# A two-block transformer kernel in split fp32: the feed-forward norm's factor applied after the products instead of before

## What is computed

```python
def rmsnorm(x, g):
    xf = x.astype(jnp.float32)
    y = xf * lax.rsqrt(jnp.mean(xf * xf, axis=-1, keepdims=True) + EPS)
    return (y * g.astype(jnp.float32)).astype(x.dtype)
...
        x = x + merged @ w_o[l]

        h = rmsnorm(x, norm_ffn_g[l])
        gt, up = jnp.split(h @ w_ffn_in[l], 2, axis=-1)
        x = x + (jax.nn.silu(gt) * up) @ w_ffn_out[l]
```

## Time and profile before

| | us |
|---|---|
| median of 3 runs | 1573.46 |
| lowest, highest | 1570.94, 1575.38 |
| the profiled execution, its time | 1571.23 |
| the profiled execution, its span | 1569.4 |

### The profile page before, as it was taken

How to read it: one execution, slowest core, us unless ns; L and a number is a source line. 1 busy time by engine, 2 the same in 40 slices (tenths; PEclk the granted TensorE clock), 3 DMA queues, 4 the chain that set the end, 5 groups by cost and what they waited for, 6 DMA issues and landing times. The chain is left out here.

```text
span 1569.4 us, 25089 instructions
## 1 busy us (share of the span) xinstructions
PE 1524.5 (97%) x10118; PEld 1342.1 (86%) x10118; DVE 1149.5 (73%) x1497; ACT 819.5 (52%) x1113; POOL 131.5 (8%) x119
## 2 busy tenths in 40 slices
PE   7999999999999999999998989999999999999998
PEld 6999889999799988999987678887888888878887
DVE  6798678786678867878569777777878766766665
ACT  6464454444646445444468755445656565655442
POOL 2060000000113000000004000000111102000000
PEclk9999999999999999999999999999999999999999
DMA  9765366666775646667632247766887765346652
GB/s 327 263 222 202 134 232 229 205 239 240 249 269 202 203 134 232 201 218 274 236 128 96 93 171 269 259 223 193 288 289 251 267 168 187 108 150 211 211 171 102
DMA packets 223762, 327.42 MB, mean 209 GB/s; under 512 B 12216, under 2 KB 175520, under 8 KB 223648
## 3 DMA queue, kind: packets, MB, share of 16 engines
q1 hardware_dynamic: 216584, 315.11, 59.6%
q10 hardware_dynamic: 7064, 10.71, 1.9%
HBM read 316.32 MB, written 9.47 MB: 208 GB/s over the span
## 5 line engine op out<-in xcount | busy, mean ns | idle before, releaser
L1768 DVE TENSOR_TENSOR wparts<-raw,wparts 128x2048 fp32r<-128x2048 f32 (+1 forms) x240 | 545.7, 2279 | 209.7 <-ACT wparts L1285 209.5
L1285 ACT ACTIVATE wparts<-raw 128x2048 fp32r<-128x2048 f32 (+1 forms) x240 | 454.5, 1897 | 118.9 <-PE bank L566 86.3
L564 PE MATMUL bank<-hT,wparts 128*128 128x256 f32 x1216 | 349.1, 287 | 1.7 <-DVE hT L1869 1.5
L565 PE MATMUL bank<-hT,wparts 128*128 128x256 f32 x1216 | 344.3, 283 | 0.0
L566 PE MATMUL bank<-hT,wparts 128*128 128x256 f32 x1216 | 344.3, 283 | 0.0
L564 PEld LDWEIGHTS bank<-hT,wparts 128*128 128x128 f32 x1216 | 233.1, 192 | 6.3 <-issue 6.0
L565 PEld LDWEIGHTS bank<-hT,wparts 128*128 128x128 f32 x1216 | 233.4, 192 | 0.2
L566 PEld LDWEIGHTS bank<-hT,wparts 128*128 128x128 f32 x1216 | 233.3, 192 | 0.0
L564 PE MATMUL bank<-wparts,aT 128*128 128x512 f32 (+1 forms) x536 | 212.8, 397 | 0.7 <-DVE aT L1849 0.5
L565 PE MATMUL bank<-wparts,aT 128*128 128x512 f32 (+1 forms) x536 | 208.0, 388 | 0.0
L566 PE MATMUL bank<-wparts,aT 128*128 128x512 f32 (+1 forms) x536 | 207.7, 388 | 0.0
(11 more groups left out here) (284 smaller groups left out, 1882.3 us busy)
## 6 DMA issues: line engine op xcount, KB each, us to landing
raw<-in_mlp_w SPq DMA_DIRECT2D x64, 1024.0 KB, 5.5
ada_raw<-in_ada_w SPq DMA_DIRECT2D x96, 512.0 KB, 6.4
raw<-in_w_ffn_in SPq DMA_DIRECT2D x44, 1024.0 KB, 5.3
raw<-in_w_in SPq DMA_DIRECT2D x43, 1024.0 KB, 5.7
raw<-in_dil_w_in SPq DMA_DIRECT2D x64, 512.0 KB, 4.9
raw<-in_w_ffn_out SPq DMA_DIRECT2D x22, 1024.0 KB, 5.3
raw<-in_w_o SPq DMA_DIRECT2D x8, 1024.0 KB, 5.0
biasb<-head_bias ACTq DMA_DIRECT2D x16, 512.0 KB, 6.6
```

The costliest lines, as they stand in the source:

```text
L564: pe.matmul(dst, held[:, 0, :], streamed[:, 0, :], start=start, stop=False)
L565: pe.matmul(dst, held[:, 0, :], streamed[:, 1, :], start=False, stop=False)
L1285: act.activation(view(whi[c % SPL], c), view(raw[c % RAW], c), ACT.Copy).then_inc(s_hi, 1)
L1768: dve.tensor_tensor(view(wlo[c % SPL], c), view(raw[c % RAW], c), view(whi[c % SPL], c).bitcast(F32), ALU.subtract).then_inc(s_lo, 1)
```

## The change

Per feed-forward layer of the first block:

- The norm's factor is no longer applied to x. TensorE transposes plain `x` (`raw_block`): columns 0 to 511 before output chunk 3, columns 512 to 1023 of token half 0 behind it, of token half 1 inside the first gate chunk (`first_gate`, `upper_blocks`). `hT` holds x times the gain.
- The factor is still formed from the same squares, but later in each engine's program. TensorE spreads it over all partitions with two small matmuls between the halves of the first up chunk (`spread_rstd`), and VectorE copies it into `rstd_rows`.
- Gate: ScalarE copies the sum out of PSUM (Copy in place of Silu), VectorE multiplies it by `rstd_rows` in SBUF, ScalarE takes Silu in place. The up sum is not scaled; the missing factor enters at the final addition, a `scalar_tensor_tensor` in place of a `tensor_tensor`.
- The transposes and sums use other PSUM banks, so that none is written before it is free.
- SyncE's wait ahead of the seven small loads is on the factor (`s_rstd`) in place of normed x.

```diff
@@ -803,13 +805,57 @@
                 four_for_weights()
+
+                def raw_block(k, t, b=None):
+                    nm = ("nrm", 2 * l + 1, k)
+                    if b is not None:
+                        begin("a", nm, freed_by=(s_hlo, low_done(2 * l + 1, k // 2)), b=b)
+                    return pe.transpose(bank[jobs[nm][2]][:, P * t:P * t + P], x[:, t, P * k:P * k + P], ident[:, :])
+
                 for c in range(4):
                     out_half, half = divmod(c, 2)
+                    if c == 0:
+                        sums, turned = list(rings["w"]), list(rings["a"])
+                    if c == 3:
+                        for t in range(TT):
+                            emptied(pe, ("WO", l, 0, t))
+                        for k in range(DK // 2):
+                            raw_block(k, 0, turned[k])
+                            end(raw_block(k, 1), ("nrm", 2 * l + 1, k))
                     w = weights(("WO", l, c))
                     wide_half(("WO", l, out_half), ("WO", l, c), w, half, None if out_half else ("mg", l))
-                three_for_weights()
-                norm(2 * l + 1, xnf)
+                emptied(pe, ("WO", l, 1, 0))
+                for k in range(DK // 2, DK):
+                    raw_block(k, 0, (sums[0], sums[1], turned[0], turned[1])[k - DK // 2])
+                rings.update(w=[sums[2], sums[0], sums[1]], a=[turned[2], turned[3], sums[3], turned[0], turned[1]])
+                n.update(w=0, a=0)
                 accs = None
+
+                def upper_blocks():
+                    emptied(pe, ("WO", l, 1, 1))
+                    for k in range(DK // 2, DK):
+                        end(raw_block(k, 1), ("nrm", 2 * l + 1, k))
+
+                def first_gate(name, w):
+                    bk = begin("w", name)
+                    for ks in (range(DK // 2), range(DK // 2, DK)):
+                        for i in range(2):
+                            for k in ks:
+                                await_pair(("nrm", 2 * l + 1), i, k)
+                                m = mm3(bk[:, S * i:S * i + S], w[:, :, k, P * i:P * i + P], hT[:, :, k, :],
+                                        (i, k) == (0, 0), (i, k) == (1, DK - 1))
+                            if (i, k) == (0, DK // 2 - 1):
+                                upper_blocks()
+                    end(m, name)
+
+                def spread_rstd():
+                    at = RSTD_OF[2 * l + 1]
+                    pe.wait_ge(s_rstd, at + 2)
+                    bk = begin("a", ("rstd", l))
+                    for t in range(TT):
+                        m = pe.matmul(bk[:, P * t:P * t + P], rstd[:, (at + t) % 2, 0:1].broadcast_to([P, P]), ident[:, :],
+                                      start=True, stop=True)
+                    end(m, ("rstd", l))
 
...
@@ -828,8 +874,10 @@
                             w = weights((nm, l, c))
-                            feature_major((nm, l, c), w, (0, P), hT, 0, DK,
-                                          first_of=None if c or i else ("nrm", 2 * l + 1))
+                            if c or i:
+                                feature_major((nm, l, c), w, (0, P), hT, 0, DK, between=idle if c else spread_rstd)
+                            else:
+                                first_gate((nm, l, c), w)
                             used((nm, l, c))
...
@@ -1137,7 +1185,7 @@
                     l = name[1]
-                    sp.wait_ge(s_xn, 2 * (2 * l + 1) + 2)
+                    sp.wait_ge(s_rstd, RSTD_OF[2 * l + 1] + 2)
                     for dst, a in ((posb[:, :], A["positions_2"][0:1, :].broadcast_to([96, S])), (thr[:, :], A["thr"]),
...
@@ -1494,11 +1538,22 @@
                         h_high(mg[:, 2 * kp:2 * kp + 2, :], hT_hi[:, 2 * kp:2 * kp + 2, :], 0.5)
-                for c in range(4):
+                def ffn_gain(k):
+                    return colA[:, c_ffn(l) + k:c_ffn(l) + k + 1]
+
+                def out_square(half, t):
+                    emptied(act, ("WO", l, half, t))
+                    square(2 * l + 1, 2 * half + t, sqf, t, half, 512 * half, 512 * half + 512)
+
+                for c in range(3):
                     split_ahead(("WO", l, c))
-                norm_sums(2 * l + 1, sqf)
-                norm_upper(2 * l + 1, xnf)
-                norm_high(2 * l + 1, lambda k: colA[:, c_ffn(l) + k:c_ffn(l) + k + 1])
+                out_square(0, 0)
+                out_square(0, 1)
+                norm_high(2 * l + 1, ffn_gain, range(DK // 2))
+                split_ahead(("WO", l, 3))
+                out_square(1, 0)
+                norm_high(2 * l + 1, ffn_gain, range(DK // 2, DK))
+                out_square(1, 1)
 
...
@@ -1524,10 +1579,12 @@
                             emptied(act, ("UP", l, c - 2))
-                        act.activation(sg[c % 2][:, :, :], bk[:, :].rearrange("p (a s) -> p a s", a=2), ACT.Silu)\
+                        act.activation(sg[c % 2][:, :, :], bk[:, :].rearrange("p (a s) -> p a s", a=2), ACT.Copy)\
                            .then_inc(drain_sem(("GT", l, c)), 1)
                         split_ahead(("UP", l, c))
                         stage_biases(u0)
+                        act.wait_ge(s_scaledgate, NF1 * l + c + 1)
+                        act.activation(sg[c % 2][:, :, :], sg[c % 2][:, :, :], ACT.Silu).then_inc(s_silu, 1)
                         emptied(act, ("UP", l, c))
...
@@ -2094,20 +2151,25 @@
                 split_ahead(("AO", l, 1))
+                def ffn_gain(k):
+                    return colA[:, c_ffn(l) + k:c_ffn(l) + k + 1]
+
                 for c in range(3):
                     split_ahead(("WO", l, c))
                     if c == 0:
                         continue
                     half = c - 1
+                    if half:
+                        norm_out(2 * l + 1, ffn_gain, (0, 1))
                     for t in range(TT):
                         nm = ("WO", l, half, t)
                         bk = full(dve, nm)
                         xs = x[:, t, 512 * half:512 * half + 512]
                         dve.tensor_tensor(xs, xs, bk[:, :], ALU.add).then_inc(drain_sem(nm), 1)
-                        if (half, t) == (1, 0):
-                            norm_mean(2 * l + 1, 0)
-                norm(2 * l + 1, xnf)
-                norm_out(2 * l + 1, lambda k: colA[:, c_ffn(l) + k:c_ffn(l) + k + 1])
+                norm_out(2 * l + 1, ffn_gain, (2, 3))
+                split_ahead(("WO", l, 3))
+                for t in range(TT):
+                    norm_mean(2 * l + 1, t)
 
...
@@ -2151,8 +2213,15 @@
                         split_ahead(("UP", l, c))
+                        if c == 0:
+                            bk = full(dve, ("rstd", l))
+                            dve.tensor_copy(rstd_rows[:, :], bk[:, 0:S]).then_inc(drain_sem(("rstd", l)), 1)
+                            emptied(dve, ("rstd", l))
+                        emptied(dve, ("GT", l, c))
+                        dve.tensor_tensor(sg[c % 2][:, :, :], sg[c % 2][:, :, :],
+                                          rstd_rows[:, :].unsqueeze(1).broadcast_to([P, 2, S]), ALU.mult).then_inc(s_scaledgate, 1)
                         steps_of(u0 + 3)
-                        emptied(dve, ("GT", l, c))
+                        dve.wait_ge(s_silu, NF1 * l + c + 1)
                         nm = ("UP", l, c)
...
@@ -2173,7 +2242,8 @@
                     xs = x[:, t, 512 * half:512 * half + 512]
-                    dve.tensor_tensor(xs, xs, bk[:, :], ALU.add).then_inc(drain_sem(nm), 1)
+                    dve.scalar_tensor_tensor(out=xs, in0=bk[:, :], scalar=rstd[:, (RSTD_OF[2 * l + 1] + t) % 2, 0:1], in1=xs,
+                                             op0=ALU.mult, op1=ALU.add).then_inc(drain_sem(nm), 1)
                     if q == 2:
```

More of the change, by code:

```diff
@@ L184, in block_pair @@
             sqf = sb("sqf", [P, D], at=ph)
-            xnf = sb("xnf", [P, TT, D], at=ph)
+            rstd_rows = sb("rstd_rows", [P, S], at=ph)
             sg = [sb(f"sg{i}", [P, 2, S], at=ph) for i in range(2)]
@@ L272, in block_pair @@
         s_sumq, s_sumk = sem("query_squares_summed"), sem("key_squares_summed")
+        s_scaledgate, s_silu = sem("gate_scaled"), sem("gate_activated")
         s_x2, s_mg, s_scaled = sem("x_updated"), sem("branches_merged"), sem("weights_gated")
@@ L382, in block_pair @@
         RSTD_OF = (0, 6, 8, 14, 16, 28, 30, 56)
-        TURN_EARLY = {e: (0, 1, 2, 3, 4, 5, 6, 7) if e == 0 else (0, 1, 3, 4, 5, 6, 7) if e in (1, 3) else
-                      (0, 1, 2, 3, 4, 5, 6) if e == 5 else (0, 3, 4, 5) if e == 7 else (0, 1, 2, 3, 4, 5) for e in range(8)}
+        TURNED_AT = {0: 0, 2: 1, 4: 2, 5: 3, 6: 4, 7: 5}
+        TURN_EARLY = {e: (0, 1, 2, 3, 4, 5, 6, 7) if e == 0 else (0, 1, 2, 3, 4, 5, 6) if e == 5 else (0, 3, 4, 5) if e == 7 else (0, 1, 2, 3, 4, 5) for e in range(8)}
         def low_done(e, kp):
@@ L636, in choose_slab_banks @@
             def choose_slab_banks():
```

(25 more changed lines are left out.)

## The result

| | before | after |
|---|---|---|
| median of the runs | 1573.46 us (1570.94 to 1575.38, 5 runs) | 1588.06 us (1585.85 to 1591.03, 5 runs) |
| profiled execution, its span | 1571.23, 1569.4 us | 1587.37, 1585.4 us |
| mean granted TensorE clock | 0.996 | 0.990 |

The changed kernel is slower: the ratio of after to before is 1.0093, with a 95% interval of 1.0081 to 1.0105. The forecast was 1589 in 1583 to 1597. The two spans differ by 16.0 us, and all of it has arisen where the first down chunk of layer 1 starts, 617.76 before and 633.77 after. The rest of the program keeps its pace. At the start of layer 0's output projection the new kernel is 0.2 us ahead, and at that of layer 1's it is 7.28 behind; these two shifts are taken off wherever a time of after is set beside one of before.

The account below looks back on a forecast made before the run. TensorE, busy 97%, was taken as the bound, fed just in time by a chain from one DMA issue. 2 x (7.9 + 0.1) = +16 us on the profiled 1571.2 gave 1587.2, as a median 1589, range 1583 to 1597.

Parts of the forecast that it names:

- the promise: Net gain from TensorE's shorter hole at the feed-forward norm, less the factor's spread: 2.65 us a layer.
- step 4: VectorE's chain after the second gate chunk: 1.8 us of new gate work; first down chunk starts 7.9 us later.
- Step 1: TensorE's hole between output projection and first gate chunk shrinks from 5.05 to 2.1 us; net 2.65 a layer.
- the sign that named 1.5 us for it: Expected sign: the first gate matmul starts about 1.5 us after the last output matmul.
- Steps 2 and 3: Layer 1: factor complete at 598.5, so small loads 6.3 us later; TensorE stands 7.4 us, second gate chunk starts 4.7 later.
- Step 5: ScalarE's table load, between the second up chunk's split and the Silu: hidden, 0; on the path, +1.3 a layer.
- Step 6: The other 20 chunks: 0.69 us more VectorE work each, covered by 3.4 us to spare; 0.1 a layer.
- Step 7: Cold TensorE behind the new wait: 0 in the sum, hidden in the down chunk's wait; bound +1.6 us a layer.
- A: Rival: second gate chunk's weights come in time, each layer gains 2.65 us, 1568 us; chance 0.07.
- The limit of 593.2: Latest issue time of the second gate chunk's load at which the rival of a kept promise could hold.
- B: Rival: only the wait for the second gate chunk reaches TensorE, cost 9.4 us, 1583 us; chance 0.05.
- C: Rival: VectorE bounds the whole stage, 14 us more over 20 chunks, 1603 us; chance 0.05.

Follow-up runs that it names:

- run 1: Changed kernel with SyncE's wait ahead of the seven small loads moved early, to the low parts of the merged branches: 1566.01 us, ratio 0.9952.
- run 3: Kernel before with SyncE's wait moved early, to the low parts of the merged branches: 1571.09 us, ratio 0.9987.
- run 7: Changed kernel with early queue and one-step gate (Silu straight from PSUM, no multiplication by the factor): 1565.51 us, ratio 0.9960.
- run 6: Changed kernel with 60 unused transposes keeping TensorE busy before the second gate chunk: 1589.92 us, ratio 1.0110.
- run 4: Changed kernel with one-step gate: Silu straight from PSUM, no multiplication by the factor, spread kept: 1584.99 us, ratio 1.0070.
- run 9: Changed kernel with both the one-step gate and the 60 dummy transposes: 1583.18 us, ratio 1.0066.
- run 2: Kernel before with its queue held until VectorE has split the first up chunk: 1586.33 us, ratio 1.0085.
- run 8: Changed kernel with both means ahead of VectorE's split of the first up chunk, and that split waiting for POOL's powers: 1582.88 us, ratio 1.0068.
- run 5: Changed kernel with VectorE's two means moved ahead of its split of the first up chunk: 1586.19 us, ratio 1.0088.

## Why the prediction was right, by its steps

With the queue as a second axis the medians read:

| queue released | before | after | the change is worth |
|---|---|---|---|
| early, in both | 1571.09 | 1566.01 | -5.1 |
| as each kernel has it | 1573.46 | 1588.06 | +14.6 |
| late, in both | 1586.33 | 1588.06 | +1.7 |

"Late" is the first up chunk's low part in the kernel before and the factor in the changed one, two events that leave the queue waiting 23.4 and 22.9 us a layer. With the queue late the promise is gone as well: everything up to the down chunk then counts from the arrival of the second gate chunk, and a TensorE that is there earlier only waits longer. TensorE of the kernel before in layer 0, for step 4:

```profile
220.07 0.36 PE L564 MATMUL bank<-hT,wparts 128*128 128x256 f32 x1 [0.28 <-DVE h L2158]
...
226.04 0.47 PE L564 MATMUL bank<-wparts,aT 128*128 128x512 f32 x1
```

- **Step 1, the hole: right.** The step matmuls were to start at 603.1 in before's time (597.0 + 5.8 + 0.3) and do at 610.38 - 7.28 = 603.10. The first gate matmul comes 0.36 us behind the last transposes, near the step's 0.45; the sign that named 1.5 us for it did not agree with the step and did not come. The gain of 5.1 us shows only with the weights in time (runs 1 and 3).
- **Steps 2 and 3, factor and queue: right.** Forecast 598.5 for the small loads, measured 598.13; forecast 7.4 us of standing, measured 7.38 and 7.81; forecast 4.7 later for the second gate chunk, measured 4.6 in layer 0 (218.22 + 0.2 against 213.78) and 5.1 in layer 1. Layer 1 has more because its seven loads took 3.47 us (605.41 to 608.88) instead of 2.82, the one of `relb` alone 1.07.
- **Step 4, the chain: right in its sum, wrong in the place of the wait.** From the split of the second gate chunk to the first hidden product VectorE took 626.75 - 616.20 = 10.55 us, against 610.97 - 602.25 = 8.72 before: 1.83 more, forecast 1.8. What failed is the sentence "TensorE, done with the second up chunk at 623.15, waits another 2.5 us". That wait is 0.21 us. TensorE is held one chunk earlier (the up chunk starts at 627.58 - 7.28 = 620.30, where the step has 617.35): the second up chunk needs the bank of the first up sum, which is free only when `h` has been formed from it, and `h` is late by the same chain. From `h`, one up chunk of 5.8 us lasts nearly as long as VectorE's steps to the end of the down chunk's split (626.75 to 633.52, start to end), so both ways lead to nearly the same start of the down chunk, and the sum did not notice. That is luck: the path through the bank was not in the sum, and the sign "2 to 3 us at the first down chunk" did not come. The kernel before already touched this limit: its second up chunk of layer 0 waits 0.28 us for `h`. I had followed the weights alone, and no bank. The down chunk came 7.4 us later in layer 0 (233.24 + 0.2 against 226.04) and 8.7 in layer 1, 16.1 in all, forecast 15.8.
- **Step 5, the table load: right.** It ends at 621.80, and the Silu starts at 626.08.
- **Step 6, the other chunks: right.** The shift is 16.0 at layer 1's first down chunk and 16.0 at the end, and between runs 1 and 7 lie 0.5 us, inside the spread of their runs.
- **Step 7, the lower clock: right that it costs nothing, but its size and its cover were misread.** The bound was 1.6 us, and the chunk lost 2.4 (8.4 instead of 6.0). It hid not in a wait for the down chunk but in that for `h` (layer 0 of run 6); with that cover gone, one layer of two pays 1.0 (runs 4 and 9), and run 2 up to 2.2 in both together. The Trainium skill (TensorE: Matmul & The Clock Gate, Part 1), cited there, says that an idle TensorE drops to 1.2 GHz; here the granted clock agrees, 0.50 behind the wait.
- **Rivals.** A is what run 1 gives (1566 against its 1568), but its condition, an early issue, did not hold. The limit of 593.2 was also set too late: for a down chunk 2.65 us earlier, behind a chain 1.8 longer with 0.25 to spare (617.51 to 617.76), the issue must come 4.2 us earlier, at 590.8. B (1583) fell with step 4: the chain's new steps do reach TensorE, since run 4, without them, is 3.1 us faster. C (1603) fell with run 7.

## What to carry to other kernels

When a value moves to a later point, look up everything that waits for it, the DMA queues above all: here one wait for a small thing also held back every large load queued behind it (runs 1 and 2). Let a queue wait for the last use of the memory that it writes, not for an event that happens to be about then; here that one line decides between 0.9% slower and 0.5% faster than before. And when such a chain is late, follow the PSUM banks as well as the weights, since the consumer stops at whichever is ready last.

## What the runs showed of the hardware

**A large VectorE instruction held POOL's short ones up.** Two powers of 128x1 took 1.09 us with VectorE idle or on 128x1 work (changed kernel, run 8) and 2.82 us beside its 128x2048 split, a subtraction of two SBUF inputs (run 5; in run 1 too, at 205.30, with the split at 205.42, where only TensorE's spread of the factor waited for them, at 208.17, for some 0.2 us). The queue's start moved with them. In both the second power ended 0.42 us after the split did. The Trainium skill (SBUF — State Buffer, SBUF: two separate sides) says that VectorE and GpSimd share one pair of ports: of a GpSimd instruction and a VectorE one with two SBUF inputs, whichever starts first takes the pair for its whole length, and the other fully blocks. The rows agree for the second power. For the first they show nothing: it began 0.12 us ahead of the split, and yet the split took its usual 2.28 us. The two powers are one group in the trace, so the second one's own start is not seen. I had priced run 5 by the 1.09 us alone.

**The table load doesn't wait for its instruction's operand.** It ran at 620.52, 5.6 us ahead of the Silu that it serves, while the Silu waited for VectorE. In run 1 it lies 7.6 us ahead (207.69 and 215.30).

**The same stretch of idleness was paid back at different speeds.** After 7.4 to 8.1 us of standing, the second gate chunk ran 8.4 us in layer 0 of the changed kernel and 8.0 in layer 1 (618.55 to 626.53); in run 4 layer 1 lost about 1 us less than layer 0. After waits of 3.06 and 3.04 us for `h` in run 6, the granted clock stayed at 1.00 in layer 0 and fell to 0.50 in layer 1. One layer's figure for a lower clock is not the other's.
